# Each block's mixer between the expert phases: a two-layer hybrid trunk taken in blocks of 128 tokens

## The reference

```
hn = rms_norm(h, norm1_g[layer])
proj = hn @ w_in[layer]                       # 1024 x 2824, split into three head groups
o_a = gdn_mixer(...)                          # gated delta rule: conv, triangular inverse of (1 + L), state
o_b = s5_mixer(...)                           # diagonal state space model, a scan over the tokens, a gated unit
o_c = diff_attn_mixer(...)                    # causal differential attention
h = h + concat(o_a, o_b, o_c) @ w_out[layer]
h = h + peer_ffn(rms_norm(h, norm2_g[layer]), peer_wq, peer_keys, peer_u, peer_v)
```

## Time and profile before

| | us |
|---|---|
| time, median of 3 runs (lowest to highest) | 2094.53 (2093.51 to 2096.13) |
| span of the profiled execution | 1904.2 |
| median less span | 190.3 |
| PE busy in the span | 1439.1 |
| DVE busy | 1266.6 |
| POOL busy | 965.5 |
| ACT busy | 371.0 |

### The profile page before, as it was taken

One profiled execution on the slowest core, in us unless ns is written; L12 is line 12 of the kernel. 1 busy time (PEld: TensorE's weight loads), 2 busy tenths in 40 slices (PEclk: granted clock), 3 DMA queues, 4 the chain that ended last, 5 costly groups with the idle time before them and its releaser, 6 DMA issues.

```text
span 1904.2 us, 19447 instructions
## 1 busy us (share of the span) xinstructions
PE 1439.1 (76%) x4688; PEld 822.1 (43%) x4688; DVE 1266.6 (67%) x3338; ACT 371.0 (19%) x950; POOL 965.5 (51%) x1028
## 2 busy tenths in 40 slices
PE   6898878776677776677988888787667777667777
PEld 5776764332233332233466677642223333223333
DVE  6967565767777766777278683656777766777671
ACT  2023212111121111111210332121111111111112
POOL 0000046777777777777200000567777777777771
PEclk9898888888888888888998999888888888888889
DMA  7230058999999999999921200789999999999993
GB/s 314 89 111 1 1 192 352 420 420 420 420 411 414 406 416 406 403 417 404 375 89 68 89 1 1 280 350 416 403 409 412 410 393 420 414 410 396 404 405 153
DMA packets 154703, 586.18 MB, mean 308 GB/s; under 512 B 17168, under 2 KB 17168, under 8 KB 149520
## 3 DMA queue, kind: packets, MB, share of 16 engines
q0 software_dynamic: 147456, 536.94, 70.2%
q1 hardware_dynamic: 7184, 48.51, 6.7%
HBM read 584.33 MB, written 1.05 MB: 307 GB/s over the span
## 4 chain that ended last, share of the span: by engine, by line
PE 64%; DVE 24%; DVEq 3%; DMA 3%; issue 3%; ACT 2%; ACTq 0%; SPq 0%; POOL 0%; PEldq 0%; POOLq 0%
PE ps L385 63%; DVE big L1236 13%; DMA big<-in_v_tab,small 1%; DMA big<-in_u_tab,small 1%; PE ps L388 1%; DVE big L1081 1%; DVEq L1085 1%; ACT sel L1460 1%; DVE big L1084 1%; DMA keysT<-in_keys 0%; DVE small L1044 0%; DVE small L1248 0%; DVE big L873 0%; DVE scores L870 0%; DVE big L867 0%
## 5 line engine op out<-in xcount | busy, mean ns | idle before, releaser
L385 PE MATMUL ps<-big,sel 128*128 128x512 f32 x2048 | 939.4, 621 | 345.5 <-ACT sel L1460 343.0
L1473 POOL DMA_INDIRECT big<-in_u_tab,small x512 | 480.8, 939 | 710.3 <-issue 660.4
L385 PEld LDWEIGHTS ps<-big,sel 128*128 128x128 f32 x2048 | 407.1, 201 | 877.8 <-issue 508.4
L1236 DVE CUSTOM_DVE_ANT_0 big<-big,ps 128x1024 f32<-128x1024 f32 x512 | 593.7, 1217 | 58.5 <-DMA big<-in_u_tab,small 49.1
L1473 POOL DMA_INDIRECT big<-in_v_tab,small x512 | 484.5, 946 | 192.6 <-issue 124.4
L1460 ACT ACTIVATE sel<-cst,small 128x128 f32<-128x128 f32 x512 | 195.7, 399 | 591.5 <-PE ps L385 564.1
L1223 DVE TENSOR_SCALAR small<-small 128x16 uint32<-128x16 f32 x32 | 7.5, 234 | 293.4 <-PE ps L385 293.1
L385 PE MATMUL ps<-hnT,big 128*128 128x256 f32 (+1 forms) x800 | 183.9, 389 | 11.3 <-ACTq L1302 6.8
L385 PEld LDWEIGHTS ps<-hnT,big 128*128 128x128 f32 x800 | 153.2, 197 | 39.4 <-ACTq L1302 8.4
L385 PE MATMUL ps<-big 128*128 128x128 f32 (+3 forms) x776 | 102.0, 308 | 8.3 <-DVEq L1085 6.0
L385 PE MATMUL ps<-big,hnT 128*128 128x256 f32 x448 | 105.1, 395 | 0.0
(11 more groups left out here) (263 smaller groups left out, 1009.3 us busy)
## 6 DMA issues: line engine op xcount, KB each, us to landing
big<-in_w_blocks SPq DMA_DIRECT2D x38, 1024.0 KB, 5.0
big<-in_u_tab,small POOLq DMA_INDIRECT x512, 6.2
big<-in_v_tab,small POOLq DMA_INDIRECT x512, 6.2
cols<-in_cols SPq DMA_DIRECT2D x2, 1085.0 KB, 6.6
rows<-in_rows SPq DMA_DIRECT2D x2, 998.0 KB, 9.2
h<-in_x SPq DMA_DIRECT2D x1, 1024.0 KB, 5.2
keysT<-in_keys SPq DMA_DIRECT2D x2, 512.0 KB, 10.5
out<-hn SPq DMA_DIRECT2D x2, 512.0 KB, 3.2
```

The lines of the kernel that those rows point to most:

```text
L385: return nc.tensor.matmul(o, a, b, start=start, stop=stop, skip_group_check=True)
L1236: V.tensor_tensor_reduce(uring[:, k, :], uring[:, k, :], xt, 1.0, 0.0, ALU.mult, ALU.add, dots[:, t, k:k + 1]).then_inc(dot_done.sem, 1)
L1473: nc.gpsimd.indirect_dma_start(dst, None, table, bass.IndirectOffsetOnAxis(ap=index, axis=0)).then_inc(done.sem, 16)
```

## The change

The program is written anew, for the same mathematics, with the weights in the same blocks. It takes the tokens in blocks of 128: there are four blocks (`NI`), layer 0 tokens 0 to 127, layer 0 tokens 128 to 255, and the same two of layer 1. Each block has a mixer (`mix(i)` and `attention(i)`) and an expert phase of four head pairs.

- The mixer of a block streams all 19 weight blocks, each in two halves (`CHUNKS`, 512 KB, ring `WRING` of four), and multiplies with 128 tokens: most fills have 128 columns where they had 256. The weights are so read four times in the kernel, not twice.
- The convolution moves from DVE to PE (24 matmuls with diagonal matrices `convm`, which ACT makes), the masks and subtractions of the inverse and of the attention move from DVE to PE too (a matmul with the identity starts each sum), and many copies move to ACT.
- The S5 tables and sums are those of 128 tokens with a carried state; `y_part` has outputs of 32 partitions (128x32 weights).
- An expert phase goes by pairs of heads: 32 u rows and 32 v rows for each pair n. POOL issues u of pair n and v of pair n - 1 in turn. Rings: six u rows (`URING`), eight v rows (`VRING`).
- A gather of v now takes the rows of 4 tokens for 32 slots (the ids are transposed in 32x32 blocks); PE multiplies each with weights of 128x32 (`wmat`), and the four gathers of a group write four different quarters of 32 output partitions (`values`).
- Where the mixer's steps stand: every step has a place in a list of slots (`place`), and `Stages.advance` runs all whose place is reached. Slots under 33 are run beside the dots of the block before; all others get 128 added, which is past the last slot of the phase, and are run after it.
- All loops are written out; there is no hardware loop.

The core of the diff:

```diff
+URING, VRING, WRING = 6, 8, 4
+END = 1.0e9
+def place(i, slot):
+    return slot if slot < 33 else slot + PAIR * 4
+class Stages:
+    def advance(self, limit):
+        while self.parts:
+            part = min(self.parts, key=lambda one: one[1])
+            if part[1] > limit:
+                return
+            part[1] = next(part[0], END)
...
 # PE
+        def values(m, i):
+            first_, fresh = 32 * m + 4 * i, m % 4 == 0 and i == 0
...
+            for c in range(4):
+                pe.wait_ge(v_in[(first_ + c) % VRING].sem, 16 * ((first_ + c) // VRING + 1))
+            for half in range(2):
+                for c in range(4):
+                    g = 4 * i + c
+                    ins = mm(bank(2 + half)[32 * c:32 * c + 32, :], wmat[:, m % 2, 32 * g:32 * g + 32],
+                             vring[:, (first_ + c) % VRING, 512 * half:512 * half + 512], fresh)
+                    if half == 1:
+                        ins.then_inc(v_used.sem, 1)
...
+        stages = Stages(mix(0), attention(0))
+        stages.advance(END - 1)
+        for n in range(NP + 1):
...
+            for j in range(PAIR):
+                if n > 0 and j % 4 == 3:
+                    values(n - 1, j // 4)
+                stages.advance(PAIR * (n % 4) + j)
+            if n % 4 == 3:
+                stages.advance(END - 1)
...
 # POOL
-            u_rows(layer, n, t, range(TOPK))
-            v_rows(layer, n, t, range(TOPK))
+        for n in range(NP + 1):
+            if n < NP:
+                pool.wait_ge(ids_ready.sem, n + 1)
...
+                    if q >= URING:
+                        pool.wait_ge(dot_done.sem, q - URING + 1)
...
+                    gather(uring[:, q % URING, :], u_tab, ids[n % 2][:, j:j + 1], u_in[q % URING])
+                if n > 0:
+                    q = 32 * (n - 1) + j
+                    if q >= VRING:
+                        pool.wait_ge(v_used.sem, q - VRING + 1)
...
+                    gather(vring[:, q % VRING, :], v_tab, idv[(n - 1) % 3][:, j:j + 1], v_in[q % VRING])
...
 # DVE, steps of mix(i) with their slots
+            if t == 0:
+                yield place(i, 2)
+                for k in tables(i):
+                    yield place(i, k)
+            if i >= TB:
+                yield place(i, 32.5)
+                add_y(i - TB)
+            if i > 0:
+                yield place(i, 34)
+                norm1(i)
```

More of the change, by code:

```diff
@@ L215, in _build @@
[L215 to L231, removed]
+    carry = tiny(2 * MT).rearrange("p (r m) -> p r m", r=2)
+    first = tiny(2 * MT).rearrange("p (r m) -> p r m", r=2)
+    ab = tiny(8)
+    beta, hbeta, gg, ga, gb_, ea, ngc, eg = (tiny(4) for _ in range(8))
@@ L233, in _build @@
+    ab_u = tiny(64, U32)
+    ab_f = tiny(64)
+    eij = tiny(64)
+    idf, idT = tiny(32), tiny(32)
+    ids = [tiny(32, U32) for _ in range(2)]
+    idv = [tiny(32, U32) for _ in range(3)]
+    gate = tiny(32).rearrange("p (h k) -> p h k", h=2)
+    gz, rgz = tiny(2), tiny(2)
+    gh = [tiny(32) for _ in range(2)]
+    dots, ge, gt, dh, pk, pkT = (tiny(32) for _ in range(6))
+    jk = tiny(64)
     ps = ctx.enter_context(nc.psum_tensor("ps", [P, 8, 512], F32))
@@ new lines, in mix, with attention @@
+            yield place(i, 100)
+            dve.wait_ge(*sd_ready(i, 2))
+            V.reciprocal(rstd, rstd)
+            fence()
+            V.scalar_tensor_tensor(hn[:, :], h[:, t, :], rstd, row("g2"), ALU.mult, ALU.mult).then_inc(hn2_ready.sem, 1)
+            k = 109
+            for _ in top(4 * i):
+                yield place(i, k)
+                k += 0.65
+            yield place(i, 121)
+            gates(4 * i)
+        def attention(i):
+            t, layer = i % 2, i // 2
+            rs = rounds(i)
+            yield place(i, 65)
+            dve.wait_ge(*y_ready(i, 4))
+            for half in range(2):
+                V.scalar_tensor_tensor(s5y[:, half, :], uT[:, half, :], col("dsk")[:, half:half + 1], s5y[:, half, :],
+                                       ALU.mult, ALU.add)
@@ new lines, in _ @@
+        V.tensor_scalar(const("lev"), const("lev"), -1.0, None, ALU.mult)
+        V.drain().then_inc(cst_ready.sem, 1)
+        stages = Stages(mix(0), attention(0))
+        stages.advance(END - 1)
+        for n in range(NP):
+            if n % 4 == 0:
+                b = n // 4
+                stages = Stages(mix(b + 1), attention(b + 1)) if b + 1 < NI else Stages(final_first())
+            choose = top(n + 1) if n % 4 != 3 else iter(())
+            next(choose, None)
+            for j in range(PAIR):
+                dot(n, j)
+                if j == 0 and n > 0:
+                    weights(n - 1)
+                if 2 <= j < 23 and (2 * j) % 3 != 1:
+                    next(choose, None)
+                if j == 26 and n % 4 != 3:
+                    gates(n + 1)
+                if j == PAIR - 1:
+                    gelu(n)
+                stages.advance(PAIR * (n % 4) + j)
+            if n % 4 == 3:
+                stages.advance(END - 1)
@@ new lines, in att_second, with att_copy @@
+        def att_second(i, r, h0, nh):
+            pr = probs(i % 2)
+            act.wait_ge(att_rz.sem, r + 1)
+            for hd in range(h0, h0 + nh):
+                copy(pr[:, hd, 1, :], pr[:, hd, 1, :], lrz[:, hd:hd + 1])
+            S.drain().then_inc(att_p1.sem, 1)
+        def att_copy(i, r, last, o):
+            act.wait_ge(pT_done.sem, r + 1)
+            g0 = 4 if i % 2 and last else 0
+            copy(pT[:, g0:g0 + 4, :], o.rearrange("p (g q) -> p g q", g=4)).then_inc(pT_ready.sem, 1)
@@ L1470, in _ @@
+        final(1)
     @block.gpsimd
```

2235 lines of the change are left out of this document (1168 added, 1067 removed).

## The result

The changed kernel takes **2270.5 us** (median of 4 runs, 2260.9 to 2271.9), the kernel before 2094.0 beside it: ratio 1.082, 95% interval 1.079 to 1.085. It is slower, as forecast, but 110 us under the 2381 predicted and 50 under the range. The profiled execution took 2271.0 us with a span of 2269.2: 1.8 us lie outside it, and 1.8 to 1.9 in the three other runs, not 190.

A forecast was written before the change was run, and what follows sets the result against it. PE and hand-offs bound the mixers, gather transfers the expert phases. Mixers 805, phases 1324 and last part 62 gave a span of 2191 us; with 190.3 between span and median, 2381, range 2320 to 2490.

The forecast's parts named there:

- the 190.3 between span and median: Time outside the traced span, added to the 2191 us span; assumed to stay with a longer program.
- The low end: Four mixers at 182 and a tail of 57, written 2381 - 44 - 5 = 2332, taken to 2320 us.
- PE too late for the v ring: Rival in the phases: v rows released 3.0 us late in each of 120 groups, 360 in all, 2741; chance 0.05.
- A: Mixer stage from the last dot to the first fill: 9.5 us.
- B: Mixer stage from the fills to the first level: 71 us, PE work of 69.
- C: Mixer stage of six levels: 44 us, with attention's PE work of 8 and 7 for ACT's queue.
- D: Mixer stage of solve, state, norm and transposes: 8.6 us, PE nearly idle.
- E: Mixer stage of the output projection: 32 x 0.448 = 14.3 us.
- F: Mixer stage from residual to ids: 39.5 us, with a top for two heads of 17.5.
- the 6 added for the clock: Allowance in each mixer for a granted clock of 0.91, raising the stage sum of 186.9 to 193 us.
- the 8 added for a wider attention and the carried state: Second block of a layer: 6 of PE work and 2 of ACT more, 201 us for 193.
- Beside after all: Rival: PE runs into the next mixer while POOL streams; up to 199 us each, three hidden give 1784; chance 0.03.

## Why the prediction was right and wrong

*"With the 190.3 between span and median": failed; with the mixers, below, it cost the range.* There is no such thing. Time and span differ by 1.8 us in every run; the trace shown was of an execution at the level of 1900, and the times of one at 2094. The 190 lie in the phases. I said that nothing priced it, gave it no rival and no part of the range, and named only the sign by which it would show. The Trainium skill, Runtime: NRT & Kernel Launch, The ~15µs preamble/postamble breakdown, has a gap of about 6.2 us between a profile's total and the time the runtime reports, with the total the longer of the two; here the time is 1.8 longer than the span, and by either 190 was no overhead. That page spoke against my step, and I had not weighed it.

That the step did not cost more is luck. The changed kernel has a lateness of its own in its phases, 139 us (1460.6 for 1321.8 in the table), which stood in for the 190: 50 too much is left. The mixers were 65 too much, the last part 6.5 too little, the phases 2 too much: 110 together. The low end was also added up wrongly: four mixers at 182 are 728, 77 under 805 and not 44, which makes it 2299; the mixers came to 740.

*The span of 2191.* At the level of its own trace the changed kernel has 2132.5:

| | forecast | at 1900 | at 2094 |
|---|---|---|---|
| mixers | 805 | 740.8 | 740.1 |
| phases | 1324 | 1321.8 | 1460.6 |
| last part | 62 | 69.9 | 68.5 |
| span | 2191 | 2132.5 | 2269.2 |

*Phases, right.* Pairs of 64 gathers at 1.28, the first pair at DVE's pace and 9 for the tables give 1324, 2 us more than measured at 1900. The lateness of the other level could not be read from a trace that has none. By its form it is my rival "PE too late for the v ring", named by the same waits, but not for its reason: PE's matmuls end in time and the count is late. It cost 139 where the rival had 360. The Trainium skill, Perfetto Trace Analysis, Summary: the profiler window per engine type, says that a matmul's end is estimated and that the time its semaphore takes to be seen is hidden. By that rule a row's end is not the release; here the trace agrees, with 5.7 us between them at one level, and some 0.1 at the other.

*Mixers, right in kind, 65 too much.* PE's work was 142 forecast for the third and is 148.7 with a burst of v rows (3.6) in it, so that term was no lower than forecast, and yet the whole is shorter: the third takes 178.7 for 193. Its stages, on the timeline:

```profile
1093.90 3.64 PE L401 MATMUL ps<-vring,wmat 128*32 128x512 f32 x16 [9.67 <-DMA vring<-in_v_tab,small]
1098.84 1.09 PE L404 MATMUL ps<-cst,hn 128*128 128x128 f32 x8 [1.30 <-ACT hn L1308]
1100.82 5.47 PE L401 MATMUL ps<-hnT,wring 128*128 128x128 f32 x32 [0.88 <-ACTq L1405]
...
1168.81 1.13 PE L401 MATMUL ps<-cst 128*128 128x512 f32 x2
...
1210.95 1.10 PE L401 MATMUL ps<-nat,gd 128*128 128x64 f32 x8 [0.69 <-ACT gd L1308]
...
1219.29 14.59 PE L401 MATMUL ps<-wring,hnT 128*128 128x256 f32 x56 [0.69 <-ACT hnT L1308]
...
1240.49 3.43 PE L401 MATMUL ps<-cst,hn 128*128 128x128 f32 x16 [4.42 <-DVE hn L1060]
```

From the last dot (1093.77): A 7.0 (9.5 forecast), B 68.0 (71), C to 1210.3 some 41 (44), D 9 (8.6), E to 1236 16.8 (14.3), F to 1272.49 36.4 (39.5). Each stage was close; four of the six (A, B, C, F) were 2.5 to 3 high, and of the 6 added for the clock 2.5 came, in E: 14 together. These 14 stand in the second and fourth mixer too, which are 21 and 19 short of the forecast. The rest there is the 8 added for a wider attention and the carried state: they cost 1 and 3 over the third, and 5 and 6 at the level of 1900 (181.75 and 183.17 against 176.69). The first is 11 short, though DVE's tables did show:

```profile
43.91 0.21 ACT L1422 ACTIVATE small<-small 128x4 f32<-128x4 f32 x1 [10.89 <-DVEq L983]
...
47.91 0.59 PE L401 MATMUL ps<-small,cst 128*128 128x4 f32 x2 [9.49 <-ACT gd L1308]
```

DVE is at the tables until 43.2, ACT waits for what DVE does next, and PE for ACT: 9.5, where 8 were forecast. Its 11 are the same stages, and 16.8 of loading for 19. So the mis-sized terms are the hand-offs of A, B, C and F and the allowance for the clock, taken four times.

*Last part, 7 low.* I had 11.3 us for two groups (release 2.1, four issues 4.2, landing 5); the bursts of the changed kernel there start at 2228.4, 2242.8 and 2256.8 with one between each, 14 us for two.

```profile
2228.43 3.64 PE L401 MATMUL ps<-vring,wmat 128*32 128x512 f32 x16 [5.54 <-DMA vring<-in_v_tab,small]
2232.83 0.94 POOL L1621 DMA_INDIRECT vring<-in_v_tab,small  x1 [4.56 <-PE ps L401]
...
2236.55 0.94 POOL L1621 DMA_INDIRECT vring<-in_v_tab,small  x1 [0.30 <-issue]
...
2242.75 3.64 PE L401 MATMUL ps<-vring,wmat 128*32 128x512 f32 x16 [5.12 <-DMA vring<-in_v_tab,small]
```

From burst to release 4.4, to the fourth issue 3.7, to the next burst 6.2. Two terms were mis-sized: the release (4.4 for 2.1, since packed products end together) and the landing (6.2, as in the earlier trace rows, for 5).

*"Beside after all", rightly refused:* nothing of a mixer runs while gathers do. Its price was right in kind: three hidden were put at up to 597 with three mixers of 199; they are 542 long and 394 net.

*Direction, right, and for its reason.* At 1900 the changed kernel's four mixers take 232.6 us more than the two before (740.8 for 508.2), and its phases with the last part 4.3 less (1391.7 for 1396.0): nothing is paid back. At 2094 the mixers take 231.9 more and the phases 58 less (1529.1 for 1587.0), since the level costs the kernel before more; hence 1.082 there for 1.120. The edit of the placement alone costs 394 us at 1900 (1738.6 to 2132.1) and 417 at 2094. With its mixers beside, the rewrite is 161 us under the kernel before at 1900. My sum priced the two together.

## What to carry to other kernels

Before a span and a set of times are put into one sum, see that they are of one level: here a difference of 10% between span and median was no overhead but another execution. Run the unchanged kernel together with the variant, or a change of level passes for an effect of the edit. And a mixer put beside a stream of gathers is worth its length less what its matmuls and DVE steps hold up the rings, here 131 of 180 us. Rows for one ring should not be taken from another that something on the path waits for: both u rows and weights cost more than they gave.

## What was not expected of the hardware

The kernel before has two levels, 1900 and 2097 on one chip, each steady to 0.6% through the runs taken together. At the upper one counts from PE come late while u and v gathers run: in one burst of three all four together, by up to 6.6 us, in the burst before it some of them, and DVE has unnamed idle of up to 7.3 us (at most 0.5 in the changed kernel at 1900). In the last part, with v gathers alone, counts are prompt. The late bursts come with a period of three, 34.7 us, in which POOL loses some 5 us. The upper level was met three times (2094.0, 2093.7, 2097.4 for the kernel before) and the lower twice (1899.7, 1901.7). No experiment here could switch it.

The traces hold one more mark of it. At the upper level, records of counts are missing: the changed kernel's trace there has 256 of the 512 counts of dots and 401 of those of v rows, its trace at 1900 has all, and so it is in every kernel here (256 to 328 of the dots at the upper level, all at the lower); blocks of weights that land while no gather runs have all their records at either level. Every run here was recorded by the profiler, so nothing shows whether the upper level would be there without it. What sets the level, and what holds the counts, is not settled.

Packed products of 32 columns left PE mostly at 1.2 GHz in the phases (0.54 to 0.60 granted), the same products one by one brought it to 0.88 in the last three, and the mixers had 0.90 to 0.95 in both cases.
